# Token mixing of a recurrent block regrouped: one factor on ScalarE, the other on VectorE

## What is computed

```python
prev = jnp.concatenate([shift0.astype(F32)[:, None], p[:, :-1]], axis=1)
xm = p + (prev - p) * lp['rwkv_mu']
r, k, v, xw, xa, xg = jnp.split(xm, RWKV_SPLITS, axis=-1)
w = -jax.nn.softplus(-(lp['rwkv_w0'] + jnp.tanh(xw) @ lp['rwkv_w2'])) - 0.5
a = jax.nn.sigmoid(lp['rwkv_a0'] + xa @ lp['rwkv_a2'])
g = jax.nn.sigmoid(xg) @ lp['rwkv_g2']
kk = _l2norm(_heads(k * lp['rwkv_k_k'], HEAD_DIM))
```

## Time and profile before

| what | value |
|---|---|
| median of three runs | 1550.01 us |
| the profiled execution | 1553.8 us |
| its span | 1551.9 us |
| mean granted TensorE clock | 0.954 of full |
| TensorE, VectorE, ScalarE, GpSimd busy | 92%, 56%, 48%, 10% |
| DMA queue of the weights | 35.5% of the 16 engines |

### The profile page before, as it was taken

The page is one execution under the profiler, slowest core; times in us unless marked ns, Lnnn a source line. Parts: engine busy times, 40 slices in busy tenths (PEclk is TensorE's granted clock), DMA queues, the critical chain, the costliest instruction groups (busy, mean ns, idle before and its releaser), DMA issues. The chain is left out here.

```text
span 1551.9 us, 31737 instructions
## 1 busy us (share of the span) xinstructions
PE 1425.8 (92%) x12552; PEld 1377.0 (89%) x12552; DVE 873.2 (56%) x1370; ACT 748.3 (48%) x965; POOL 147.8 (10%) x166
## 2 busy tenths in 40 slices
PE   6999998799977899999989999987897788999997
PEld 5999998788965899999989999987897668999996
DVE  4555435886565665553365554358856554655533
ACT  6666433633335465553366653354432445655432
POOL 1000001221222000000010000022122121000000
PEclk9999999889978999999999999998998889999999
DMA  6444443312102434454444444431230024544441
GB/s 240 162 149 149 151 149 107 109 48 84 50 2 69 151 124 158 140 157 149 149 150 148 149 150 149 149 102 62 81 96 16 3 74 147 172 152 146 152 149 46
DMA packets 50766, 185.86 MB, mean 120 GB/s; under 512 B 5760, under 2 KB 6272, under 8 KB 50176
## 3 DMA queue, kind: packets, MB, share of 16 engines
q1 hardware_dynamic: 49104, 177.37, 35.5%
q10 hardware_dynamic: 1584, 7.35, 1.4%
HBM read 180.14 MB, written 4.56 MB: 119 GB/s over the span
## 5 line engine op out<-in xcount | busy, mean ns | idle before, releaser
L448 PE MATMUL ps<-xh,wh 128*128 128x320 f32 x1952 | 619.9, 318 | 40.2 <-DVE xl L1269 33.9
L449 PE MATMUL ps<-xl,wh 128*128 128x320 f32 x1952 | 612.1, 314 | 0.0
L450 PE MATMUL ps<-xh,wl 128*128 128x320 f32 x1952 | 611.6, 313 | 0.0
L1256 DVE TENSOR_TENSOR wl<-raw,wh 128x1024 fp32r<-128x1024 f32 x332 | 407.4, 1228 | 279.3 <-ACT wh L955 279.2
L955 ACT ACTIVATE wh<-raw 128x1024 fp32r<-128x1024 f32 x332 | 349.3, 1055 | 402.7 <-PE ps L450 388.7
L448 PEld LDWEIGHTS ps<-xh,wh 128*128 128x128 f32 x1952 | 374.8, 192 | 50.0 <-issue 29.9
L449 PEld LDWEIGHTS ps<-xl,wh 128*128 128x128 f32 x1952 | 375.0, 192 | 0.8
L450 PEld LDWEIGHTS ps<-xh,wl 128*128 128x128 f32 x1952 | 374.6, 192 | 0.0
L448 PE MATMUL ps<-hid_h,wh 128*128 (+1 forms) x704 | 217.9, 310 | 4.0 <-DVE hid_l L1289 4.0
L450 PE MATMUL ps<-hid_h,wl 128*128 (+1 forms) x704 | 217.5, 309 | 0.0
L449 PE MATMUL ps<-hid_l,wh 128*128 (+1 forms) x704 | 217.5, 309 | 0.0
(11 more groups left out here) (278 smaller groups left out, 1201.4 us busy)
## 6 DMA issues: line engine op xcount, KB each, us to landing
raw<-wts SPq DMA_DIRECT2D x332, 512.0 KB, 3.5
ms<-mst ACTq DMA_DIRECT2D x2, 1440.0 KB, 6.6
mout<-ms ACTq DMA_DIRECT2D x2, 1440.0 KB, 6.7
x<-xT SPq DMA_DIRECT2D x4, 320.0 KB, 6.7
yT<-x SPq DMA_DIRECT2D x4, 320.0 KB, 2.2
cs<-cst SPq DMA_DIRECT2D x1, 650.0 KB, 9.7
pr<-par ACTq DMA_DIRECT2D x1, 429.0 KB, 3.2
pr<-par ACTq DMA_DIRECT2D x1, 425.0 KB, 5.5
```

Source lines behind the costliest of these rows:

```text
L448: pe.matmul(out, a, rh, start=start, stop=False)
L449: pe.matmul(out, a, rl, start=False, stop=False)
L450: return pe.matmul(out, b, rh, start=False, stop=stop)
L1256: tt(wl[:, s, :], raw_of(layer, n), wh[:, s, :].bitcast(F32), ALU.subtract).then_inc(lo_ready.sem, 1)
```

## The change

`rw_mix` no longer subtracts. ScalarE writes (1 - mu) times the tile into `xm` (`own_part(k)`, two activations with a per-partition scale, prompt and sample), and VectorE adds mu times the shifted tile, in two instructions per place of the form that it had. The factor 1 - mu is computed by one 128x7 operation on VectorE ahead of the projection's first eviction (`mu_rest`, a new buffer `rest`). The order of ScalarE's parts is `SCALED`: own part 6 stands between `ahead(1)` with the table load and `ahead(2)`; own parts 2 and 3 ahead of `ahead(3)`; own part 0 ahead of `ahead(4)` and own part 1 behind it; own parts 4 and 5 ahead of `ahead(7, 8, 9)`. Each own part waits for the count of `in_read` of its tile. VectorE's mixing of place k waits for the k-th own part (`xm_own`). The settling waits ahead of and behind the subtractions go, the one at the end stays.

```diff
--- before.py
+++ after.py
@@ -51,6 +51,7 @@
             + [GLA0 + 128 * i for i in range(4)] + [RG0 + 128 * i for i in range(2)]
             + [GDN0 + 3 * GW + 128 * i for i in range(2)] + [GLA0 + 128 * i for i in range(4, 6)]
             + [RG0 + 128 * i for i in range(2, 4)])
+SCALED = (6, 2, 3, 0, 1, 4, 5)
 LATE = 14
 
 
@@ -107,7 +108,7 @@
 
 
 MIX_SIGNALS = {
-    "padded": ("pads", "chain_zero", "rg_pads"), "xm": 7, "lora_in": 1, "lora_mm": 3, "sg": 2, "ra": 2,
+    "padded": ("pads", "chain_zero", "rg_pads"), "mu_rest": 1, "xm_own": 7, "xm": 7, "lora_in": 1, "lora_mm": 3, "sg": 2, "ra": 2,
     "rw_gc": 2, "shift_kept": 1, "kkraw": 2, "kk_sq": 1, "rkr": 2, "head_sums": ("kk_sum", "rk_sum", "gdn_sum"), "cum": 2, "prev": 1,
     "rw_P": 1, "kk_rn": 1, "rb": 1, "rw_ops": 1, "kPi": 1, "bPi": 1, "bonus": 1, "kbL": 4,
     "rw_pairs": 2, "rw_pairs_read": 6,
@@ -123,7 +124,7 @@
     "yo": 3, "yo_dec": 3, "ysq0": 1, "ysq1": 1, "ysq2": 1, "yrs": 2, "mean_mm": 1, "mean_read": 1, "var_mm": 3, "VM": 6, "dec_mm": 3,
     "dec_decay": 3, "var_read": 2, "dec_add": 3, "sq_sum": 3,
 }
-V_STEPS, A_STEPS, G_STEPS = 121, 32, 16 + 3 * 6
+V_STEPS, A_STEPS, G_STEPS = 113, 39, 16 + 3 * 6
 
 
 class Signal:
@@ -197,6 +198,7 @@
         rstd = sb("rstd", [128, TOK])
         lnt = sb("lnt", [128, TOK])
         tiny = sb("tiny", [128, 16])
+        rest = sb("rest", [128, 7])
 
         with nc.sbuf_tensor("hid_h", [128, FT, TOK], F32R) as hid_h, \
                 nc.sbuf_tensor("hid_l", [128, FT, TOK], F32R) as hid_l, \
@@ -1039,11 +1041,22 @@
                     on(act, layer, "R0_mm", g + 1)
                     say(act.activation(rstd[:, 0:256] if g == 0 else A(72, 256), ps[:, 6 + g, 0:256], ACT.Copy), "R0T")
 
-                ahead(1, 2)
+                def own_part(k):
+                    if k == 6:
+                        on(act, layer, "mu_rest")
+                    on(act, layer, in_read, RW_ORDER.index(k) + 1)
+                    st(act.activation(xm[:, k, 0:SEQ], rwp[:, k, 1:1 + SEQ], ACT.Copy, scale=rest[:, k:k + 1]))
+                    say(act.activation(seqs(xm[:, k, :], 0), seqs(rwp[:, k, :], 1, 1), ACT.Copy, scale=rest[:, k:k + 1]), "xm_own")
+
+                ahead(1)
                 act.preload_act_table_set("sigmoid_and_others")
+                own_part(6)
+                ahead(2)
                 act.wait_ge(S["xm"].sem, S["xm"].upto(layer, 1))
                 st(act.activation(xm[0:32, 6, :], xm[0:32, 6, :], ACT.Tanh))
                 say(act.activation(xm[64:128, 6, :], xm[64:128, 6, :], ACT.Sigmoid), "lora_in")
+                own_part(2)
+                own_part(3)
                 ahead(3)
                 act.wait_ge(in_read.sem, in_read.upto(layer, T_SMALL + 1))
                 say(act.activation(small[0:NH, :], small[0:NH, :], ACT.Sigmoid), "beta")
@@ -1055,7 +1068,9 @@
                 on(act, layer, "lora_mm", 2)
                 for p in range(2):
                     say(act.activation(ra[:, p, :], ps[:, 6 + p, 0:TOK], ACT.Sigmoid, bias=P("a0", p)), "ra")
+                own_part(0)
                 ahead(4)
+                own_part(1)
                 act.preload_act_table_set("natural_log_exp_and_others")
                 R = slice(32, 32 + NH)
                 st(act.activation(tiny[R, 10:11], P("alog")[R], ACT.Exp))
@@ -1086,6 +1101,8 @@
                 say(act.activation(lnt[R, :], lnt[R, :], ACT.Ln, bias=C("one")[R]), "sp_dt")
                 say(act.activation(tiny[:, 11:13], tiny[:, 11:13], ACT.Ln, bias=C("one")), "sp_lam")
                 say(act.activation(ltm, ltm, ACT.Ln, bias=C("one")), "gla_ln")
+                own_part(4)
+                own_part(5)
                 ahead(7, 8, 9)
                 on(act, layer, "rw_rows_mm", 1)
                 st(act.activation(rVt[:].rearrange("q c p t -> q (c p) t"), banks(2, (0, 10)), ACT.Copy))
@@ -1329,13 +1346,10 @@
                 def rw_mix(lo, hi):
 
                     on(ve, layer, "pads")
-                    st.settle()
-                    st(tt(xm[:, lo:hi, 0:SEQ], rwp[:, lo:hi, 0:SEQ], rwp[:, lo:hi, 1:1 + SEQ], ALU.subtract))
-                    st(tt(seqs(xm[:, lo:hi], 0), seqs(rwp[:, lo:hi], 1, 0), seqs(rwp[:, lo:hi], 1, 1), ALU.subtract))
-                    st.settle()
                     for k in range(lo, hi):
-                        st(stt(xm[:, k, 0:SEQ], xm[:, k, 0:SEQ], P("mu", k), rwp[:, k, 1:1 + SEQ], ALU.mult, ALU.add))
-                        say(stt(seqs(xm[:, k, :], 0), seqs(xm[:, k, :], 0), P("mu", k), seqs(rwp[:, k, :], 1, 1), ALU.mult, ALU.add), "xm")
+                        on(ve, layer, "xm_own", SCALED.index(k) + 1)
+                        st(stt(xm[:, k, 0:SEQ], rwp[:, k, 0:SEQ], P("mu", k), xm[:, k, 0:SEQ], ALU.mult, ALU.add))
+                        say(stt(seqs(xm[:, k, :], 0), seqs(rwp[:, k, :], 1, 0), P("mu", k), seqs(xm[:, k, :], 0), ALU.mult, ALU.add), "xm")
                     st.settle()
 
                 def rw_keys_raw():
@@ -1689,6 +1703,7 @@
                 ffn(layer, 0)
                 norm_low(layer, 1, "nm", 0.5)
                 ahead(0)
+                say(ts(rest[:], P("mu", 0, 7), -1.0, 1.0, ALU.mult, ALU.add), "mu_rest")
                 on(ve, layer, rstd_ready, 2)
                 ve.wait_ge(unit_used.sem, layer * UNITS + IN0)
                 evac(0)
```

## The result

The changed kernel takes 1558.5 us, the median of five runs (1557.5 to 1559.3), against 1550.0 us: a ratio of 1.0057 with a 95% interval of 1.0041 to 1.0073. It is slower, by 6 to 11 us. The forecast was 1559.6 us.

What follows compares the result with a forecast made beforehand. The prediction took VectorE's eviction of tile 7 plus a fixed 4.1 us on GpSimd to set TensorE's restart. Delays summed to 4.8 us per layer, 9.6 us in all, from 1550.0 to 1559.6 us; range 1555 to 1564.

Steps and rivals of the forecast that it cites:

- Place 6: At tile 6 VectorE waits for ScalarE's own part 6 and starts its multiply-add 1.5 us late, despite 0.60 us less work.
- the raw keys: Behind places 2 and 3, 0.93 us is won back on VectorE, so the raw keys start 0.45 us late.
- the split of number 4: Own part 0 stands ahead of this ScalarE split, so VectorE's low split of tile 8 starts 1.1 us late.
- The step that decides: ScalarE's own part 1 waits for VectorE's eviction of tile 5; VectorE's low split of number 5 comes 5.8 us late.
- The eviction of tile 7: VectorE keeps its order up to there, less 0.93 us of subtractions, so this eviction is 4.9 us late.
- The restart of TensorE: Pair products start a fixed 4.1 us of GpSimd work after VectorE's eviction of tile 7: 311.45 instead of 306.59.
- Behind it: After tile 7 VectorE idles about 1.8 us for a split; 5.2 us late after the last subtractions, hidden at tile 9.
- The margin of 1 us at tile 9: VectorE's masks end near 321.3, TensorE's tile 9 comes at 322.3, so the masks' delay hides with 1 us in hand.
- rival 1: Larger delay behind tile 7, slower VectorE uses up the slack: 1 to 2 us more per layer, 1561.6 to 1563.6; chance 0.08.
- Rival 4: Own parts ride in ScalarE's gaps; VectorE reaches the eviction of tile 7 earlier by 2.46 us: 1545.1 us; chance 0.05.
- The sum: All delays in the mixing stage together: 4.8 us per layer, 9.6 us in all, giving 1559.6 us; chance 0.76.
- Rival 2: Tile 8 keeps TensorE at 2.4 GHz into the products, 1.8 us less, 3.0 us left per layer: 1556.0; chance 0.05.

Runs made afterwards that it cites:

- own1_after_split5: The changed kernel with only own part 1 moved behind the split of number 5 on ScalarE: 1547.6 us, 0.9977 of the kernel before.
- only_place1: The kernel before with place 1 alone computed the new way, its own part at the changed kernel's position: 1558.2 us, 1.0037 of the kernel before.
- change_place6_old: The changed kernel with place 6 subtracted as before and its own part gone: 1554.8 us, 1.0023 of the kernel before.
- three runs around own part 5: Own part 5 behind splits 7 and 8 in the changed kernel (1.0041), likewise with own part 1 late (0.9999); kernel before with only places 4, 5 new (0.9991).
- parts_in_gaps: The changed kernel with place 6 subtracting, own parts 0 and 1 behind split 5, 4 and 5 behind split 8: 1544.5 us, 0.9954 of the kernel before.
- change_again: The changed kernel measured once more, unaltered, in a later group: 1558.0 us, 1.0043 of the kernel before.

## Why the prediction was right, and where a term was off

*Place 6, the raw keys, the split of number 4.* Expected 1.5, 0.45 and 1.1 us late. Against rstd the rows give 1.60 (276.56 against 276.10), 0.46 (282.17 against 282.85) and 1.10 us (286.91 against 286.95). Each own part holds ScalarE for 0.65 us (275.71 to 276.36 in the trace), as taken.

*The step that decides.* A wait of ScalarE of some 4 us before own part 1: 4.07. VectorE 5.8 us late at the low split of number 5: 295.53 against 290.87 is 5.80. The runs own1_after_split5 and only_place1 show that this place alone makes a delay of 4.4 to 4.65 us per layer at the products. Place 6 adds its 1.6 us (change_place6_old).

*The eviction of tile 7.* Expected 4.9 us late, measured 4.89 (305.69 against 301.94).

*The restart of TensorE: mis-sized.* The prediction added "a fixed 4.1 us on GpSimd" and so expected the products 4.9 us late. They are 3.45 us late (308.90 against 306.59): from the end of the eviction to the restart it is 2.7 us here, not 4.1. GpSimd's pieces aren't fixed. The shift save and the product took 3.3 us before and 1.9 us in the change, because own part 5 holds the split of number 7 up and VectorE stands still for 1.76 us just then. The prediction had foreseen this idle time to 0.04 us and had booked it as a delay that hides; it is a gain of 1.4 us per layer. The three runs around own part 5 show it.

*Behind it.* The margin of 1 us at tile 9 is gone, but not as rival 1 had it: TensorE came sooner, not VectorE later. VectorE's masks end 4.6 us late (5.2 expected) and are followed by the eviction of tile 9 without a wait (319.45; 1.44 us of waiting before), 3.1 us late. From there on the two layers stay 2.9 and 3.4 us late at the transpose, a sum of 6.3 us instead of 9.6. (The steps of the prediction give 4.87 us per layer, which its sum carries as 4.8.)

*Rival 4.* Own parts that ride in ScalarE's gaps didn't come about in the order of this change, as the prediction said. With place 6 left as it was and the others placed in the gaps (parts_in_gaps), the eviction of tile 7 does come 2.05 us earlier and the kernel takes 1544.5 and 1545.6 us. So the rival's price was about right, and the order of ScalarE's entries is what kept the change from it.

*The sum.* The median moved by 8.5 us. The two measurements of the change give 6 to 11 and 4 to 9 us, and the 6.3 us of the two stages lie within the second and at the lower edge of the first. The kernel before points to where most of the 2 us between 6.3 and 8.5 come from: its 1550.0 us rest on five runs, while 76 in the later groups have medians of 1551.3 to 1552.2 us, and change_again is 5.9 us above the median of its own group. A small cost further down isn't excluded. The range of 1555 to 1564 holds in either case, while the closeness of 1559.6 to 1558.5 is partly luck: the sum was too large by 3.3 us at the transposes, and the low median before made up for a part of it.

*The clock.* Rival 2, the clock that stays up, doesn't happen. The granted clock of the changed kernel by windows (columns as in the earlier trace rows; the figure of a window is a mean of the two levels, 1.00 for 2.4 GHz and 0.50 for 1.2):

```profile
282.00:284.00 2.00, 2.00 (x8) 1.65 (x7) 1.97 (x5) 1.11 (x3) 0.00 (x0) 0.60 0.73 254
...
298.00:300.00 2.00, 1.33 (x7) 1.36 (x8) 1.86 (x6) 1.97 (x4) 0.00 (x0) 0.86 0.75 254
300.00:302.00 2.00, 2.00 (x9) 2.00 (x9) 1.97 (x4) 1.92 (x5) 0.00 (x0) 0.50 0.00 0
302.00:304.00 2.00, 1.95 (x11) 1.69 (x9) 2.00 (x3) 1.40 (x5) 0.00 (x0) 0.78 0.00 0
304.00:306.00 2.00, 0.00 (x0) 0.00 (x0) 2.00 (x4) 0.00 (x0) 0.00 (x0) 1.00 0.45 127
306.00:308.00 2.00, 0.00 (x0) 0.00 (x0) 0.24 (x3) 1.74 (x4) 1.60 (x3) 0.57 0.33 135
308.00:310.00 2.00, 1.10 (x11) 1.13 (x13) 2.00 (x2) 0.90 (x1) 1.73 (x3) 0.50 0.02 4
```

TensorE starts tile 8 after a wait:

```profile
298.67 0.39 PE L450 MATMUL ps<-xh,wh 128*128 128x320 f32 x1 [1.97 <-DVE ar L1331]
```

That is where the prediction had it (299.8 by the times of before), but the wait is 2.0 us instead of the 3 to 4 foretold, because the tiles ahead of it were held up by a stretch at half clock (0.60 in 282 to 284) on top of the late start. Tile 8 itself then runs mostly at half clock (0.50 in 300 to 302) and ends near 303.9, where the prediction took 2.4 GHz and 3.6 us. The clock is back at 1.00 from 304 to 306; in the next window, with TensorE idle, it falls to 0.57, and the products start at 1.2 GHz (0.50). The wait before them is 4.95 us, just under the 5 to 8 foretold. They take 6.6 and 7.0 us in the two layers, 7.2 and 7.0 before. The trace agrees with the Trainium skill (TensorE: Matmul & The Clock Gate, "What's actually happening") in that the clock halves after idling and comes back with work. Over all runs the products took 5.9 to 7.5 us with the same instructions, so a layer can differ by up to 1.6 us here from one execution to the next, and from the other layer of the same execution.

## What to carry to other kernels

Work moved to an engine with spare time costs what stands behind its waits in that engine's order, not its duration. Of seven parts of 0.65 us one, waiting for a result of the engine that needed the next entry of the queue, cost most of the time lost; a second, whose result came too late for the engine that consumes it (place 6), cost 1.6 us per layer. Before moving an instruction, find for its place which result it waits for, when that comes, and who waits for the entries behind it; here a place a few entries later made the same change a small gain. And where VectorE and GpSimd both work from SBUF, don't take GpSimd's durations as fixed: they depend on what VectorE does at that moment.

## What the runs showed of the hardware

GpSimd's 128x7 copy takes 0.20 us while VectorE stands still and 1.02 us while VectorE runs a 128x1024 subtraction with two inputs in SBUF that began 0.25 us earlier; it ends with that subtraction. In the other direction the subtraction took 2.56 us instead of 1.22 when GpSimd's 128x640 product, 1.85 us long, had begun 0.38 us before it. Both agree with the Trainium skill (SBUF — State Buffer, "Who interferes with whom"): a VectorE instruction with two SBUF inputs contends with a GpSimd instruction that reads SBUF for a pair of ports that they share, the pair is an exclusive lock, and the order of issue decides which of the two is blocked. The trace of before held this too, in the copy of 1.02 us for 7 elements per partition, and the prediction passed over it.

TensorE's clock fell to half in the changed kernel from 282 on (0.60 in 282 to 284, above), where it stays at 1.00 before. In front of it TensorE had only 0.40 and 1.35 us of waiting, but between and behind these it ran only the small low-rank products (12 instructions). The same fall stands in layer 1 and in change_again. With place 6 subtracted (change_place6_old) TensorE waits only 0.23 us around the same 12 instructions, and the clock stays up:

```profile
282.00:284.00 2.00, 2.00 (x15) 2.00 (x14) 1.52 (x3) 2.00 (x5) 0.00 (x0) 1.00 0.53 211
```

In the changed kernel it didn't delay the products, since TensorE still waited 2.0 us for VectorE before tile 8.
